# Unit 0 of column pair 0 with eight plain products, and the input-tile sums formed, cast and split one by one

## The reference

```python
f = swiglu(rmsnorm(h, pre_g), w_gate, w_up, w_down)   # (2048 x 5632) twice, (5632 x 2048)
h = h + 0.5 * rmsnorm(f, post_g)
...                                                   # mixer: z = u @ w_in (2048 x 5120), RG-LRU and
...                                                   # short conv, y @ w_out (2048 x 2048)
# swiglu: (silu(x @ w_gate) * (x @ w_up)) @ w_down
```

## Time and profile before

| what | value |
|---|---|
| median of 3 runs | 1779.69 us (1779.31 to 1779.9) |
| the profiled execution's own time | 1778.62 us |
| its span, first to last instruction | 1776.8 us |
| TensorE busy | 1748.7 us, 98% |
| VectorE busy | 1292.4 us, 73% |
| ScalarE busy | 935.9 us, 53% |
| GpSimd busy | 141.0 us, 8% |
| mean granted TensorE clock | 0.997 of 2.4 GHz |
| moved by DMA | 372.14 MB, mean 209 GB/s |

### The profile page before, as it was taken

How to read it: one execution, slowest core, us unless ns; L and a number is a source line. 1 busy time by engine, 2 the same in 40 slices (tenths; PEclk the granted TensorE clock), 3 DMA queues, 4 the chain that set the end, 5 groups by cost and what they waited for, 6 DMA issues and landing times.

```text
span 1776.8 us, 22147 instructions
## 1 busy us (share of the span) xinstructions
PE 1748.7 (98%) x7826; PEld 1438.8 (81%) x7826; DVE 1292.4 (73%) x1172; ACT 935.9 (53%) x949; POOL 141.0 (8%) x129
## 2 busy tenths in 40 slices
PE   8999999999999999999999998999999999999998
PEld 6778888888888888788888876888888888888886
DVE  6989888989864444655676467889898988844444
ACT  6655555555554434656654456555555555644442
POOL 5100000000000000100000016000000000000000
PEclk9999999999999999999999999999999999999999
DMA  7777777777585556665565557777777777666554
GB/s 233 237 223 216 224 229 225 223 219 228 170 294 191 184 183 214 191 210 168 166 198 173 199 163 242 211 229 220 218 227 227 226 221 221 212 218 213 199 182 151
DMA packets 160562, 372.14 MB, mean 209 GB/s; under 512 B 12012, under 2 KB 14196, under 8 KB 159604
## 3 DMA queue, kind: packets, MB, share of 16 engines
q1 hardware_dynamic: 148948, 350.33, 60.4%
q0 software_dynamic: 11520, 20.98, 7.6%
...
HBM read 367.07 MB, written 4.19 MB: 209 GB/s over the span
## 4 chain that ended last, share of the span: by engine, by line
PE 84%; DMA 6%; DVE 5%; POOL 2%; issue 1%; ACT 1%; SPq 0%; DVEq 0%; ACTq 0%
PE ps L1242 15%; PE ps L1244 15%; PE ps L1243 15%; PE ps L1344 13%; PE ps L1346 13%; PE ps L1345 13%; DMA u_raw<-in_ffn_w_up 4%; DVE u_lo L961 1%; PE ps L1339 1%; DMA u_raw<-in_ffn_w_gate 1%; POOL x L504 1%; DVE tsum L975 1%; DVE w_lo L857 1%; ACT w_hi L562 1%; DMA raw<-in_w_in 1%
## 5 line engine op out<-in xcount | busy, mean ns | idle before, releaser
L857 DVE TENSOR_TENSOR w_lo<-raw,w_hi 128x1024 fp32r<-128x1024 f32 x316 | 395.8, 1257 | 348.9 <-ACT w_hi L562 345.3
L562 ACT CAST w_hi<-raw 128x1024 fp32r<-128x1024 f32 x320 | 335.0, 1053 | 391.3 <-PE ps L1244 341.6
L654 ACT CAST u_hi<-u_raw 128x2048 fp32r<-128x2048 f32 x160 | 305.6, 1911 | 146.2 <-DMA u_raw<-in_ffn_w_up 76.4
L961 DVE TENSOR_TENSOR u_lo<-u_raw,u_hi 128x2048 fp32r<-128x2048 f32 x160 | 364.3, 2287 | 7.0 <-ACT u_hi L654 4.1
L1242 PE MATMUL ps<-w_hi,hT_hi 128*128 128x512 f32 x832 | 324.4, 390 | 0.8 <-DVE w_lo L857 0.8
L1244 PE MATMUL ps<-w_hi,hT_lo 128*128 128x512 f32 x832 | 323.8, 389 | 0.0
L1243 PE MATMUL ps<-w_lo,hT_hi 128*128 128x512 f32 x832 | 323.6, 389 | 0.0
L1344 PE MATMUL ps<-u_hi,xT_hi 128*128 128x512 f32 x640 | 249.8, 390 | 0.4 <-DVE act_g L999 0.4
L1345 PE MATMUL ps<-u_lo,xT_hi 128*128 128x512 f32 x640 | 249.6, 390 | 0.0
L1346 PE MATMUL ps<-u_hi,xT_lo 128*128 128x512 f32 x640 | 249.5, 390 | 0.0
L661 ACT CAST t_hi<-tsum 128x1536 fp32r<-128x1536 f32 x80 | 118.6, 1483 | 154.7 <-DVE tsum L975 89.7
...
## 6 DMA issues: line engine op xcount, KB each, us to landing
...
u_raw<-in_ffn_w_gate SPq DMA_DIRECT2D x40, 1024.0 KB, 5.1
u_raw<-in_ffn_w_up SPq DMA_DIRECT2D x40, 1024.0 KB, 5.1
...
```

The lines of the kernel that those rows point to most:

```text
L562: sc.copy(w_hi[:, s], raw[:, s]).then_inc(hi_ready, 1)
L654: sc.copy(unit(u_hi, p), unit(u_raw, p)).then_inc(unit_hi, 1)
L857: ve.tensor_tensor(w_lo[:, s], raw[:, s], w_hi[:, s].bitcast(f32), ALU.subtract).then_inc(lo_ready, 1)
L961: ve.tensor_tensor(unit(u_lo, p), unit(u_raw, p), unit(u_hi, p).bitcast(f32), ALU.subtract).then_inc(unit_lo, 1)
```

## The change

In half (0, 0) of each FFN (gate, first pair) unit 0 is no longer made with sums of weight blocks: it takes eight plain products in the banks M3, M2, M5 and M4, as units 1, 3, 5 and 7 do. Its four blocks come in one DMA; its accumulating DMA, `tsum`, `t_hi` and `t_lo` are left out, and all counts of these shift by one unit per FFN. It needs a form that did not exist, D2 of unit 0 alone (128 columns). GpSimd makes the forms in a new order: D1 of the even units, D2 of unit 0, D1 and D2 of the odd units, then S1, S2 and S4. Casts and subtractions are one operation per form: forms 0 and 1 behind the split of group 13, form 2 behind that of group 14, form 3 behind that of group 15, and forms 4 to 6 behind ScalarE's cast and VectorE's subtraction of unit 0. ScalarE casts unit 0 before the Silu of gate chunk 0 in place of after it. TensorE waits before units 0, 1 and 2 for 2, 4 and 7 forms. M1, M6 and M7 start in unit 2.

```diff
@@ -102,7 +102,12 @@
         for name in (("D1", "S1", "S2", "S4") if p in SEVEN else ("D2", "D1")):
             FORM[p, name] = n_forms
             n_forms += 1
-    FORM_CUT = FORM[GP // 2, "D1"]
+    FORM_END = n_forms
+    FORM[0, "D2"] = n_forms
+    n_forms += 1
+    FORMS = [slice(FORM[p, name], FORM_END, 6) for p, name in ((0, "D1"), (1, "D1"), (1, "D2"), (0, "S1"), (0, "S2"), (0, "S4"))]
+    FORMS.insert(1, slice(FORM[0, "D2"], n_forms))
+    NF = len(FORMS)
     ROUNDS = TOK + 2 * TOK * PAIRS
     EVAC = 7
     assert FC == 2 * PAIRS + 1 and SEVEN == (0, 2, 4, 6) and NS % 2 == 0
@@ -296,18 +301,24 @@
         form_sum, form_hi, form_lo = sem("form_sum"), sem("form_hi"), sem("form_lo")
         resid_kept, resid_back = sem("resid_kept"), sem("resid_back")
 
+        def seven(q, p):
+            return p in SEVEN and (q[1] > 0 or p > 0)
+
         def unit_count(f, q, p):
             return lin(q, GP, UNITS * f + p + 1)
 
         def seven_count(f, q, n):
-            return lin(q, NS, NS * HALVES * f + n + 1)
+            return lin(q, NS, NS * HALVES * f + n + 1 - (f + 1))
+
+        def sums_count(f, q, n):
+            return lin(q, 2 * NS, 2 * (NS * HALVES * f + n + 1 - (f + 1)))
 
         def raw_count(f, q, p):
             per = 32 if p in SEVEN else 16
-            return lin(q, 2 * per, per * (UNITS // 4 * f + p // 4 + 1))
+            return lin(q, 2 * per, per * (UNITS // 4 * f + p // 4 + 1) - (16 * (f + 1) if p % 4 == 0 else 0))
 
         def pair_count(f, q, n):
-            return lin(q, 32, 16 * (NS // 2 * HALVES * f + n // 2 + 1))
+            return lin(q, 32, 16 * (NS // 2 * HALVES * f + n // 2 + 1 - (0 if n % 2 else f + 1)))
 
         def seven_used(f, q, n, back):
             n -= back
@@ -432,14 +443,16 @@
                                 else ds(it * (2 * W) + (first + b * W), n * W))
 
                     raw_u = unit(u_raw, p)
-                    if p in SEVEN:
+                    if seven(q, p):
                         n = SEVEN.index(p)
-                        if q[1] or n >= 2:
-                            sync.wait_ge(pair_used, lin(q, NS, NS * HALVES * f + n - 1))
+                        if q[1] or n > 2:
+                            sync.wait_ge(pair_used, seven_count(f, q, n - 2))
+                        elif n == 2:
+                            sync.wait_ge(unit_used, unit_count(f, q, 0))
                         sync.dma_start(raw_u[:, B12], w[:, GK * p + 1, cols(1, 1)]).then_inc(pair_raw[n % 2], 16)
                     if q[1] or p >= 4:
                         sync.wait_ge(unit_used, unit_count(f, q, p - 4))
-                    if p in SEVEN:
+                    if seven(q, p):
                         sync.dma_start(raw_u[:, B21:B22 + 1].rearrange("p n c -> p (n c)"),
                                        w[:, GK * p, cols(0, 2)]).then_inc(unit_raw[p % 4], 16)
                         sync.dma_start(raw_u[:, B11], w[:, GK * p + 1, cols(0, 1)]).then_inc(unit_raw[p % 4], 16)
@@ -506,26 +519,31 @@
                 pool.wait_ge(x32_done, NBLK * (f + 1))
 
                 def form(name, p):
-                    return xf32[:, FORM[p, name]:n_forms:6, 1]
+                    return xf32[:, FORM[p, name]:FORM_END:6, 1]
 
                 def tile(p, k, t):
                     return x32[:, 2 * p + k:KD:4, part(t)]
 
+                base = NF * f
+                pool.tensor_tensor(form("D1", 0), tile(0, 1, 0), tile(0, 1, 1), ALU.subtract).then_inc(form_sum, 1)
+                pool.tensor_tensor(xf32[:, FORM[0, "D2"], 1], x32[:, 0, part(0)], x32[:, 0, part(1)], ALU.subtract
+                                   ).then_inc(form_sum, 1)
+                pool.tensor_tensor(form("D1", 1), tile(1, 1, 0), tile(1, 1, 1), ALU.subtract).then_inc(form_sum, 1)
+                pool.tensor_tensor(form("D2", 1), tile(1, 0, 0), tile(1, 0, 1), ALU.subtract).then_inc(form_sum, 1)
                 pool.tensor_tensor(form("S1", 0), tile(0, 1, 1), tile(0, 0, 1), ALU.add).then_inc(form_sum, 1)
-                pool.tensor_tensor(form("D1", 0), tile(0, 1, 0), tile(0, 1, 1), ALU.subtract).then_inc(form_sum, 1)
-                pool.wait_ge(form_sum, 6 * f + 1)
+                pool.wait_ge(form_sum, base + 5)
                 pool.tensor_tensor(form("S2", 0), form("S1", 0), tile(0, 1, 0), ALU.subtract).then_inc(form_sum, 1)
-                pool.tensor_tensor(form("D2", 1), tile(1, 0, 0), tile(1, 0, 1), ALU.subtract).then_inc(form_sum, 1)
-                pool.wait_ge(form_sum, 6 * f + 3)
+                pool.wait_ge(form_sum, base + 6)
                 pool.tensor_tensor(form("S4", 0), tile(0, 0, 0), form("S2", 0), ALU.subtract).then_inc(form_sum, 1)
-                pool.tensor_tensor(form("D1", 1), tile(1, 1, 0), tile(1, 1, 1), ALU.subtract).then_inc(form_sum, 1)
 
             def pair_sums(f):
 
                 for q in range(HALVES):
                     for n, p in enumerate(SEVEN):
+                        if not seven((0, q), p):
+                            continue
                         first = W + 2 * W * (q // 2)
-                        pool.wait_ge(pair_raw[n % 2], 16 * (NS // 2 * (HALVES * f + q) + n // 2 + 1))
+                        pool.wait_ge(pair_raw[n % 2], pair_count(f, (0, q), n))
                         pool.dma_start(unit(u_raw, p)[:, B12], ffn_w[f][q % 2][:, GK * p + 1, first:first + W],
                                        accum_op=ALU.add).then_inc(pair_sum[n % 2], 16)
 
@@ -624,6 +642,13 @@
                     r, first = it * (2 * TOK) + r, it * (2 * MC) + first
                 hidden_copy(f, r, src, first, t)
 
+            def form_hi_of(f, *ns):
+                for n in ns:
+                    act.wait_ge(form_sum, NF * f + n + 1)
+                    sc.copy(xf[:, FORMS[n], 0], xf32[:, FORMS[n], 1]).then_inc(form_hi, 1)
+
+            FORMS_AT = {GP + 5: (0, 1), GP + 6: (2,), GP + 7: (3,)}
+
             def first_chunks(f):
 
                 pl = Place(starts[f"up{f + 1}"])
@@ -634,30 +659,28 @@
                         act.wait_ge(lam_neg, 1)
                         sc.activation(soft[:, 1], soft[:, 0], ACT.Sigmoid).then_inc(lam_sig, 1)
                     split(pl, j)
-                act.wait_ge(form_sum, 6 * (f + 1))
-                for cut in (slice(0, FORM_CUT), slice(FORM_CUT, n_forms)):
-                    sc.copy(xf[:, cut, 0], xf32[:, cut, 1]).then_inc(form_hi, 1)
+                    form_hi_of(f, *FORMS_AT.get(j, ()))
+                half_hi(f, (0, 0), 0)
+                form_hi_of(f, 4, 5, 6)
                 act.wait_ge(w_used, pl.count(GP - 1))
                 act.wait_ge(rstd_pre, 1 + 2 * f)
                 for t in range(TOK):
                     sc.activation(act_g[:, t], bank(t), ACT.Silu, scale=rstd[:, 1, t:t + 1]).then_inc(silu_done, 1)
-                half_hi(f, (0, 0), 0)
-                sums_hi(f, (0, 0), 0)
                 half_hi(f, (0, 0), 1)
 
             def half_hi(f, q, p):
                 act.wait_ge(unit_raw[p % 4], raw_count(f, q, p))
                 if q[1] == 0 and p < 2:
                     act.wait_ge(w_used, Place(starts[f"up{f + 1}"]).count(2 * GP - 3 + 2 * p))
-                if p in SEVEN:
+                if seven(q, p):
                     act.wait_ge(pair_sum[SEVEN.index(p) % 2], pair_count(f, q, SEVEN.index(p)))
                 sc.copy(unit(u_hi, p), unit(u_raw, p)).then_inc(unit_hi, 1)
 
             def sums_hi(f, q, p):
                 n = SEVEN.index(p)
-                if q[1] or n:
+                if q[1] or n > 1:
                     act.wait_ge(unit_used, seven_used(f, q, n, 1))
-                act.wait_ge(sums_done, lin(q, 2 * NS, 2 * (NS * HALVES * f + n + 1)))
+                act.wait_ge(sums_done, sums_count(f, q, n))
                 sc.copy(t_hi[:], tsum[:, (q[1] * NS + n) % 2]).then_inc(t_hi_done, 1)
 
             def m1_copy(f, q):
@@ -941,6 +964,16 @@
                 ve.tensor_tensor(hT_lo[:, tiles], hT32[:, tiles], hT_hi[:, tiles].bitcast(f32), ALU.subtract
                                  ).then_inc(hT_lo_done, 1)
 
+            def form_lo_of(f, *ns):
+                for n in ns:
+                    dve.wait_ge(form_hi, NF * f + n + 1)
+                    if n in (4, 5):
+                        dve.wait_ge(form_sum, NF * f + n + 2)
+                    ve.tensor_tensor(xf[:, FORMS[n], 1], xf32[:, FORMS[n], 1], xf[:, FORMS[n], 0].bitcast(f32),
+                                     ALU.subtract).then_inc(form_lo, 1)
+
+            FORMS_AT = {GP + 5: (0, 1), GP + 6: (2,), GP + 7: (3,)}
+
             def first_chunks(f):
                 pl = Place(starts[f"up{f + 1}"])
                 for j in range(GP, 2 * GP):
@@ -949,29 +982,25 @@
                     if f == 0 and j in (GP + 5, GP + 7):
                         softplus(("lambda", "series")[j == GP + 7])
                     split(pl, j)
-                for n, cut in enumerate((slice(0, FORM_CUT), slice(FORM_CUT, n_forms))):
-                    dve.wait_ge(form_hi, 2 * f + n + 1)
```

(30 more changed lines are left out.)

## The result

The changed kernel took 1771.59 us, the median of 6 runs (1769.51 to 1772.09), against 1779.8 for the kernel before (6 runs, 1779.31 to 1780.59): the ratio is 0.9949, with a 95% interval of 0.9938 to 0.9959, so 8.2 us or 0.5% faster. Forecast was 1772.0. Timed twice more, beside the experiments, the same kernel gave ratios of 0.9954 (0.9940 to 0.9967) and 0.9955 (0.9941 to 0.9968). The profiled execution was the fastest of its six: its own time was 1769.51 us and its span 1767.4, at a mean granted clock of 0.999. Two executions among all that follow ran far slower than the rest (one of eight_alone at 2191.1 us, one of the kernel before at 4570.32); the ratios leave them out, the medians hold them.

A forecast was written before the change was run, and what follows sets the result against it. TensorE was taken to bound the kernel, busy 1748.7 of 1776.8 us. Entry gains 0.95 + 7.4 less 0.7 make 7.7 us: 1778.62 becomes 1770.9, plus 1.07 to the median, 1772.0; range 1769.6 to 1776.4.

The forecast's parts named there:

- The stall ahead of unit 0: Both FFN entries: unit 0's `u_lo` is ready at about 56.5 and 98.4, before the chunk ends, so TensorE's wait goes.
- The delay of the split of group 15: VectorE, both entries: form subtractions ahead of the split make it later by 1.95 us (first FFN) and 3.2 us (second).
- The count of one more sum in between: VectorE, second FFN: one additional GpSimd sum gets between the operations and costs 1.1 us of the 3.2 us delay.
- Unit 2's chain: Both entries: 15.5 us from unit 1's load issue to unit 2, which starts 0.95 and 7.4 us earlier than before.
- The first term: Unit 2's B12 block lands 5.9 us after unit 1's load issue, sooner because unit 0's accumulating DMA is gone.
- The second term: Unit 2's accumulating DMA takes 5.2 us: unit 3's megabyte still runs beside it, but less lies ahead.
- The clock: Second FFN's entry: the stretch at the 1.2 GHz level disappears, worth 2.4 of the 7.4 us.
- Give-back in the loop: Second FFN's pair loop: waits for `u_lo` grow to the first FFN's, 1.5 against 0.8 us; 0.7 us off the gain.
- The late sum: Rival, chance 0.17: unit 0's missing DMA speeds nothing, unit 2's sum stays late; gain 2.5 us, time 1777.2.
- The loads did not set the pace: Rival denied here, chance 0.08: loads can't follow sooner, the second FFN's 7 us is given back; gain 0 to 2.
- The held-up queue: Rival, chance 0.05: GpSimd delays VectorE's split of group 15 by D in both FFNs; gain 12.9 - 2D, time 1781.
- The best case: Rival within the forecast's 0.70: both units 2 at TensorE's own bound, nothing given back; gain 9.8 us, time 1769.9.

The follow-up runs named there:

- eight_alone: Changed kernel with GpSimd's old order of sums, form casts and subtractions in two operations behind all splits, Silu ahead of unit 0's cast: 1776.38 us, ratio 0.9983.
- one_by_one_alone: Kernel before, seven products for unit 0 kept, with the new order of sums and forms cast and subtracted one by one between the last splits: 1777.31 us, ratio 0.9986.
- warm: Kernel before with 28 thrown-away products in TensorE's idle stretch ahead of unit 0 in the second FFN: 1777.32 us, ratio 0.9985.
- forms_behind_splits: Changed kernel with VectorE's subtractions of forms 0 to 3 behind the last split: 1769.72 us, ratio 0.9947; run again, 1770.22 us, ratio 0.9946.
- split_three_times: Changed kernel with VectorE making the split of group 15 three times in both FFNs, same result: 1775.51 us, ratio 0.9976.
- loads_2_3_first: Changed kernel with SP's loads in the order of units 0, 2, 3, 1 in the first half of each FFN: 1775.03 us, ratio 0.9972.

## Why the prediction was right, step by step

**The stall ahead of unit 0.** It goes, in both FFNs, as said. No split is late: TensorE reaches groups 14 and 15 without a wait. The parts alone show what it hung on: without unit 0's sums 4.05 us of wait remain (eight_alone), with the new order alone 4.53 (one_by_one_alone, `u_lo` behind the accumulating DMA). The parts give 3.5 and 2.6 us, together 6.1, and both at once 7.3 to 8.2. The medians' intervals alone could not tell these apart, but the entries say the same more plainly: 3.7 and 1.2 us against 7.8 to 8.4. Each part removes one of two things that end nearly together, so the second pays more once the first is gone; and either wait alone still pulled the clock down (0.57 and 0.50 behind them). The prediction priced them only together.

**The delay of the split of group 15.** Forecast 3.2 us in the second FFN and 1.95 in the first. By unit 1's load against the chunk's last product it is (1098.94 - 1092.17) - (1096.68 - 1092.73) = 2.8 us, and 1.6 in the first (there the load is issued at 53.10). The subtractions of forms 0, 1 and 2 took 3.00 + 1.70 us on the chain, far more than their 1.65 (form 1, of 128 columns, took 1.38 us beside a sum, where 0.3 was reckoned), but the two last splits fell from 2.2 and 2.3 to 1.2 us each: GpSimd's sums now met the forms and not the splits. The count of one more sum in between was about right in its total. VectorE's rows for form 2, ahead of the last split, and form 3, behind it:

```profile
1089.79 1.77 DVE L972 TENSOR_TENSOR xf<-xf,xf 128x512 fp32r<-128x512 f32 x1
...
1092.63 0.68 DVE L972 TENSOR_TENSOR xf<-xf,xf 128x512 fp32r<-128x512 f32 x1
```

The Trainium skill, page "SBUF — State Buffer", section "Who interferes with whom", has a VectorE instruction with two inputs in SBUF contend with a GpSimd instruction that reads SBUF, for a port pair that only one of them can hold. The rows agree: the same subtraction of 512 columns takes 1.77 us beside a sum and 0.68 after the last.

**Unit 2's chain.** In the second FFN:

| term | forecast | measured |
|---|---|---|
| unit 1's issue to unit 2's accumulate | 5.9 | 1098.67 - 1092.73 = 5.94 |
| accumulate | 5.2 | 1104.09 - 1098.67 = 5.42 |
| sums, cast, `u_lo`, first product | 4.45 | 1108.49 - 1104.09 = 4.40 |
| sum | 15.5 | 15.76 |

In the first FFN the sum is 69.06 - 53.10 = 15.96. The delay was 0.4 us smaller than forecast and the chain 0.3 to 0.5 longer, so the entries came out at 0.85 and 7.59 us gained, against 0.95 and 7.4. That the two errors nearly cancel is luck. The first term's reason, that the missing DMA had held up B12, holds for the first FFN (7.64 us before, 6.00 after) and is worth only 0.2 us in the second. The second term rests on weaker ground than it seemed. The forecast took 5.2 because less lies ahead; the accumulates of these kernels took 4.4 to 7.19 us, an idle one issued 8 us ahead changed nothing (5.35), and the 7.19 became 5.44 when a load moved behind it. That what was issued within some 2 us ahead of it sets its time fits most of these, but not the 6.3 us of the first FFN before, which had nothing of the weights' loads issued between 53.48 and 59.10. No run isolates it, and what sets this term stays open.

**The clock.** The granted clock is 1.00 in the second entry, as said, and warm prices that alone: 2.0 us in the trace, 2.5 by the medians, against 2.4 forecast.

**Give-back in the loop.** Forecast 0.7 us, by waits for `u_lo` that would grow to the first FFN's. They did not grow (0.8 before, 0.7 now, from 1110 to 1400 us). From unit 2 of the second FFN to the span's end there are 658.46 us before and 658.91, 658.57 and 659.0 in the changed kernel's profiles, a loss of 0.1 to 0.5 us. This is the one step whose mechanism the trace doesn't show: the waits that it was to come from did not appear, and its size is within the scatter. It was 0.7 of the forecast's 7.7 us. Without it the forecast would have been 8.4, and the medians, which gained 7.3 to 8.2, can't tell the two apart.

**The balance.** For the profiled pair: 0.85 + 7.59 in the entries, 1.47 between them, -0.45 behind them, and -0.06 ahead (the first chunk's last product at 57.26 and not 57.20) give 9.40 us, which is 1776.8 - 1767.4. The forecast of the span was 7.7. The 1.47 us was in no term, and is of the size of the scatter shown above. The median gained 8.2, 7.3 and 7.8 us.

**The rivals.** The late sum (2.5 us of gain) needed 17.8 to 18.4 us for the chain; it took 15.8 to 16.0. The loads did not set the pace: the advance of 7.6 us was kept. The held-up queue had the right exchange rate (split_three_times) with a delay of 4.4 us in both FFNs together, not 12.9. The best case was within reach of one line: forms_behind_splits has both units 2 at the bound.

**Two expectations missed,** both about the order of transfers. one_by_one_alone was to gain at most 1 us and gained 2.6, as it seems since the load no longer went ahead of the accumulate. loads_2_3_first was to gain by an earlier chain of unit 2 and lost 3.2 us, since unit 1's megabyte landed 9.0 us after its issue.
